# A hybrid decoder step on one core: the order of work at five places, and the sampled states' product with C on GpSimd

## What is computed

```python
def block(x, lp, past):
    x = x + 0.5 * swiglu(rmsnorm(x, lp["ffn1_norm"]), lp["ffn1_w_gate"], lp["ffn1_w_up"], lp["ffn1_w_down"])
    m, new_state = mix_layer(rmsnorm(x, lp["mix_norm"]), lp, past)
    x = x + m
    x = x + 0.5 * swiglu(rmsnorm(x, lp["ffn2_norm"]), lp["ffn2_w_gate"], lp["ffn2_w_up"], lp["ffn2_w_down"])
    return x, new_state
```

## Time and profile before

| | |
|---|---|
| median of three runs | 1480.89 us (1479.32 to 1481.51) |
| the profiled execution, its own time | 1479.76 us |
| its span, first to last instruction | 1477.7 us |
| PE busy | 1425.7 us, 96% |
| DVE busy | 802.8 us, 54% |
| ACT busy | 485.8 us, 33% |
| POOL busy | 194.6 us, 13% |
| chain that ended last | PE 83%, DVE 10%, ACT 3%, issue 2%, DMA 1% |

### The profile page before, as it was taken

The page is one execution under the profiler, slowest core; times in us unless marked ns, Lnnn a source line. Parts: engine busy times, 40 slices in busy tenths (PEclk is TensorE's granted clock), DMA queues, the critical chain, the costliest instruction groups (busy, mean ns, idle before and its releaser), DMA issues.

```text
span 1477.7 us, 28457 instructions
## 1 busy us (share of the span) xinstructions
PE 1425.7 (96%) x11676; PEld 1394.6 (94%) x11676; DVE 802.8 (54%) x983; ACT 485.8 (33%) x651; POOL 194.6 (13%) x187
## 2 busy tenths in 40 slices
PE   5999999999999999999999698999999999999999
PEld 5999999999999999999997688899999999999999
DVE  4444444333346557476787599885556564443222
ACT  5222232222243435342132464453332222322111
POOL 1000000010100000005700011210136750000000
PEclk9999999999999999999999899999999999999999
DMA  5232333333332313328956944556345543323332
GB/s 160 87 99 85 95 90 86 90 113 107 110 108 58 85 43 100 86 66 282 305 175 193 152 138 143 146 173 196 90 128 162 180 142 93 91 86 90 92 92 83
DMA packets 274776, 180.99 MB, mean 122 GB/s; under 512 B 13744, under 2 KB 253584, under 8 KB 274592
## 3 DMA queue, kind: packets, MB, share of 16 engines
q1 hardware_dynamic: 264512, 151.56, 36.1%
q0 software_dynamic: 6752, 22.27, 4.7%
q10 hardware_dynamic: 3456, 6.39, 1.2%
HBM read 162.42 MB, written 17.77 MB: 122 GB/s over the span
## 4 chain that ended last, share of the span: by engine, by line
PE 83%; DVE 10%; ACT 3%; issue 2%; DMA 1%; SPq 0%; DVEq 0%; ACTq 0%; POOL 0%; POOLq 0%
PE ps L442 75%; PE ps L1885 2%; DVE w_lo L423 2%; PE ps L1665 1%; PE ps L1675 1%; DVE gbuf L1294 1%; ACT w_hi L418 1%; PE ps L1681 1%; DVE hin L1283 1%; PE ps L1692 1%; DVE state L1306 1%; DVE ysm L1307 1%; DVE csb L1291 1%; DMA csb<-cs_kept 1%; PE ps L1797 0%
## 5 line engine op out<-in xcount | busy, mean ns | idle before, releaser
L442 PE MATMUL ps<-xg_hi,w_hi 128*128 128x260 f32 x2512 | 516.1, 287 | 22.2 <-DVE w_lo L423 21.7
L442 PE MATMUL ps<-xg_hi,w_lo 128*128 128x260 f32 x2512 | 508.4, 284 | 0.0
L442 PE MATMUL ps<-xg_lo,w_hi 128*128 128x260 f32 x2512 | 507.8, 284 | 0.0
L423 DVE TENSOR_TENSOR w_lo<-stage,w_hi 128x1024 fp32r<-128x1024 f32 (+1 forms) x229 | 302.0, 1319 | 264.1 <-ACT w_hi L418 260.2
L442 PEld LDWEIGHTS ps<-xg_hi,w_hi 128*128 128x128 f32 x2512 | 390.3, 190 | 28.1 <-issue 21.4
L442 PEld LDWEIGHTS ps<-xg_hi,w_lo 128*128 128x128 f32 x2512 | 389.6, 190 | 0.0
L442 PEld LDWEIGHTS ps<-xg_lo,w_hi 128*128 128x128 f32 x2512 | 389.3, 190 | 0.0
L418 ACT ACTIVATE w_hi<-stage 128x1024 fp32r<-128x1024 f32 (+1 forms) x229 | 237.3, 1036 | 330.0 <-PE ps L442 255.9
L442 PE MATMUL ps<-hid_hi,w_hi 128*128 128x260 f32 x704 | 141.9, 283 | 0.0
L442 PE MATMUL ps<-hid_hi,w_lo 128*128 128x260 f32 x704 | 141.5, 282 | 0.0
L442 PE MATMUL ps<-hid_lo,w_hi 128*128 128x260 f32 x704 | 141.3, 282 | 0.0
(11 more groups left out here) (299 smaller groups left out, 1451.0 us busy)
## 6 DMA issues: line engine op xcount, KB each, us to landing
stage<-in_w_in SPq DMA_DIRECT2D x69, 512.0 KB, 5.0
stage<-in_ffn_w_gate SPq DMA_DIRECT2D x44, 512.0 KB, 3.9
stage<-in_ffn_w_up SPq DMA_DIRECT2D x44, 512.0 KB, 3.8
stage<-in_ffn_w_down SPq DMA_DIRECT2D x32, 448.0 KB, 3.7
stage<-in_ffn_w_down SPq DMA_DIRECT2D x16, 512.0 KB, 3.9
pages<-in_cache_sb_k SPq DMA_DIRECT2D x32, 256.0 KB, 4.4
pages<-in_cache_sb_v SPq DMA_DIRECT2D x32, 256.0 KB, 3.6
gates<-gates_kept POOLq DMA_DIRECT2D x24, 260.0 KB, 4.1
```

What stands on the lines that cost most here:

```text
L423: nc.vector.tensor_tensor(w_lo[:, r, 0:kt, :], stage[:, s, 0:kt, :], w_hi[:, r, 0:kt, :].bitcast(F32), ALU.subtract).then_inc(unit_split, 1)
L442: mm = nc.tensor.matmul(out[:, h, :], wt[:, r, k, :], v[:, h * HALF:(h + 1) * HALF], start=start and k == 0 and n == 0, stop=stop and k == ...
```

## The change

- Start: SP raises its semaphores after the first loads are issued. PE runs 14 products of a matrix of ones into a bank that nobody reads, as soon as the constants stand. Unit 2 (`THIRD`) has weight buffers of its own, `w2_hi` and `w2_lo`, and is rounded before the squares; units 2 and 3 have accumulators in banks 6 and 4 of their own.
- Gates: POOL's product of a page with the query is two instructions of half the size. ACT loads the table of exponentials after the loop of gates, no longer ahead of it.
- Values: DVE copies `b_tok` one gate earlier, and takes `cb` ahead of the last convolution.
- Entry of SSD: POOL loads the decays of tile 0 earlier; ACT rounds the second unit of branch B ahead of the first decays; PE turns x after four row blocks of dense work, and does four more before the first chunk states.
- SSD loop: `csb` has three buffers, and a load runs three tiles ahead. POOL multiplies the sampled states with C; DVE waits for POOL (`state_weighted`) and only sums.

```diff
         def round_unit(u0, step, kt):
...
-            nc.scalar.wait_ge(unit_done, u0 + 1 + step)
-            nc.scalar.activation(w_hi[:, r, 0:kt, :], stage[:, s, 0:kt, :], ACT.Copy).then_inc(hi_ready, 1)
+            if u0 != THIRD:
+                nc.scalar.wait_ge(unit_done, u0 + 1 + step)
+            nc.scalar.activation(high(u0)[:, 0:kt, :], stage[:, s, 0:kt, :], ACT.Copy).then_inc(hi_ready, 1)
...
         def _(sp):
-            for s in signals:
-                sp.sem_inc(s.sem, s.n)
...
             for k in range(DT):
                 sp.dma_start(x[:, k, :], ins["x_t"][:, k, :]).then_inc(x_landed[k], 16)
...
+            for s in signals:
+                sp.sem_inc(s.sem, s.n)
...
-            act.preload_act_table_set("natural_log_exp_and_others")
             with act.Fori(0, NS // SLOTS) as i:
                 for b in range(SLOTS):
                     pass_gate(G_PRE + b, SLOTS * i)
+            act.preload_act_table_set("natural_log_exp_and_others")
...
             act.wait_ge(prep_d, 7)
+            round_unit(U_SSD + 1, 0, DT)
             decays(0, 0)
             decays(0, 1)
             for t in range(SSD_T):
                 it, u = t // 2, U_SSD + 3 * (t // 2)
-                round_unit(u + (1, 3)[t % 2], 0, DT)
+                if t:
+                    round_unit(u + (1, 3)[t % 2], 0, DT)
...
             def state_c(t):
-                dve.wait_ge(state_landed[t % 2], 16 * (t // 2 + 1))
-                dve.wait_ge(c_landed, 16 * (t // GT + 1))
-                link(nc.vector.tensor_tensor(state[t % 2][:, :, :], state[t % 2][:, :, :], cbb[:, :, :], ALU.mult))
+                dve.wait_ge(state_weighted, t + 1)
                 nc.vector.tensor_reduce(ysm[:, t, :], state[t % 2][:, :, :], AX_X, ALU.add).then_inc(state_used.sem, 1)
...
-                    nc.gpsimd.tensor_tensor(tiles, tiles, query.unsqueeze(1).broadcast_to([P, PAGES, SB_T, P]),
-                                            ALU.mult).then_inc(kq_ready.sem, 1)
+                    pair = [P, PAGES // 2, SB_T, P]
+                    for half in (tiles[:, 0:PAGES // 2], tiles[:, PAGES // 2:PAGES]):
+                        last = nc.gpsimd.tensor_tensor(half, half, query.unsqueeze(1).broadcast_to(pair), ALU.mult)
+                    last.then_inc(kq_ready.sem, 1)
...
             pool.wait_ge(cs_stored, 16)
+            load_cs(0)
             pool.wait_ge(pvd_done.sem, pvd_done.now(NS // SLOTS - 1, SLOTS - 1))
-            load_cs(0)
             load_cs(1)
+            load_cs(2)
             for t in range(SSD_T):
-                if t < SSD_T - 2:
+                pool.wait_ge(state_landed[t % 2], 16 * (t // 2 + 1))
+                pool.wait_ge(c_landed, 16 * (t // GT + 1))
+                nc.gpsimd.tensor_tensor(state[t % 2][:, :, :], state[t % 2][:, :, :], cbb[:, :, :], ALU.mult
+                                        ).then_inc(state_weighted, 1)
+                if t < SSD_T - 3:
                     pool.wait_ge(y_summed.sem, y_summed.now(0, t))
-                    load_cs(t + 2)
+                    load_cs(t + 3)
                 add_y(t)
...
             pe.wait_ge(consts_set, CONSTS)
+            for _ in range(14):
+                nc.tensor.matmul(ps[:, 7, 0:P], ones[:, :], ones[:, :], start=True, stop=True)
             ffn(1, U_FFN1A, O_FFN1A, U_FFN1B, O_FFN1B)
...
-            turn(0)
             for t in range(SSD_T):
                 dense(12 * t, 12 * t + 4)
                 if t == 0:
+                    turn(0)
...
                     mm.then_inc(v_summed, 1)
+                    dense(4, 8)
                 pe.wait_ge(xd_ready.sem, xd_ready.now(0, t))
```

More of the change, by code:

```diff
@@ L432, in multiply_unit @@
             if begin == 0:
-                if start:
+                if o0 == O_FFN1A + 3:
+                    nc.tensor.wait_ge(rms_ready, 1)
+                elif start and o0 != O_FFN1A + 2:
                     nc.tensor.wait_ge(acc_read, o0 + 1 + ostep)
@@ L439, in multiply_unit @@
                     nc.tensor.wait_ge(*ready(k))
-                for n, (wt, v) in enumerate(((w_hi, hi), (w_hi, lo), (w_lo, hi))):
+                for n, (wt, v) in enumerate(((hi_w, hi), (hi_w, lo), (lo_w, hi))):
                     for h in range(2):
-                        mm = nc.tensor.matmul(out[:, h, :], wt[:, r, k, :], v[:, h * HALF:(h + 1) * HALF],
+                        mm = nc.tensor.matmul(out[:, h, :], wt[:, k, :], v[:, h * HALF:(h + 1) * HALF],
                                               start=start and k == 0 and n == 0,
@@ L822, in decays @@
                 act.wait_ge(seg_ready.sem, seg_ready.now(0, h))
[L823 removed]
+                nc.scalar.activation(row, row, ACT.Exp).then_inc(ecs_ready.sem, 1)
                 nc.scalar.activation(gbuf[:, slot, :], gbuf[:, slot, :], ACT.Exp, scale=-1.0
@@ L1204, in _ @@
                     rest_unit(U_GATE + g + 1, SLOTS * i, DT)
+                    if i and b == 3:
+                        for k in range(GROUPS):
+                            dve.wait_ge(cb_made, k + 1)
+                            chunks = "p (c l) -> p c l"
+                            nc.vector.tensor_tensor(cb[:, k, :].rearrange(chunks, c=CH),
+                                                    ps[:, (6, 4)[k], :].rearrange(chunks, c=CH),
+                                                    upto[:, :].unsqueeze(1).broadcast_to([P, CH, P]), ALU.mult
+                                                    ).then_inc(cb_ready, 1)
                     t = ds(SLOTS * i + b, 1)
@@ L1290, in head @@
                 dve.wait_ge(ecs_ready.sem, ecs_ready.now(0, 2 * t + e))
-                nc.vector.tensor_tensor(csb[:, slot, :], csb[:, slot, :], ct[:, t // GT, :], ALU.mult
+                row = csb[t % 3][:, e, :]
+                nc.vector.tensor_tensor(row, row, ct[:, t // GT, :], ALU.mult
                                         ).then_inc(csc_ready.sem, 1)
@@ L1858, in _ @@
                         rows = slice(HD * e, HD * e + HD)
-                        mm = nc.tensor.matmul(ps[rows, 7, cols], hin[:, c, rows], csb[:, 2 * (t % 2) + e, cols],
+                        mm = nc.tensor.matmul(ps[rows, 7, cols], hin[:, c, rows], csb[t % 3][:, e, cols],
                                               start=False, stop=True)
```

73 lines of the change are left out of this document (41 added, 32 removed).

## The result

The changed kernel takes 1468.54 us (median of four runs, 1465.9 to 1469.91), the kernel before 1481.2 beside it: a ratio of 0.9913, 95% interval 0.989 to 0.9936. It is faster, by 12.7 us where 23 were forecast, and 1.5 us above the range's upper end. The profiled execution took 1469.0 us for a span of 1467.2; against that of before (1479.76, span 1477.7) it is 10.8 us shorter.

What follows compares the result with a forecast made beforehand. PE, busy 96% of the span, was bounded by few large waits, the SSD loop by DVE. Terms 9.2 + 4.5 + 13.5 - 4 = 23.2 us off gave 1457.5 us against the median, range 1447 to 1467.

Steps and rivals of the forecast that it cites:

- the range's upper end: Whole kernel: 1467 us, holding most of the exposed-product and moved-hole cases and adding the clock lost once or twice.
- Start: Start of the kernel: earlier loads, clock raised by ones, no hole before unit 2; 9.2 us off, bounds 6 and 11.
- the 1.2 for the ones: Start: products of ones raise PE's clock before the first unit; 1.2 us taken back of 2.3 lost.
- Gates: Loop of gates: the 3.15 us hole and half clock behind it go; 4.5 us off, bounds 1 and 5.
- Entry: Entry of SSD: PE's 10.86 us wait, smaller waits and half clock go, less a late head; 13.5 us off.
- What is late next is DVE's second head of tile 0: Entry of SSD: PE's next wait, its dense work ending about 1.2 us before that head.
- The prediction's own 1.2 us: Entry of SSD: PE's remaining wait for DVE's second head of tile 0, subtracted from the gain.
- The product: SSD loop: moving the product with C to POOL; 4 us on, bounds 10 off and 11 on.
- I take 1.7 us, two thirds: 1.7 - 1.22 = 0.5 a tile: SSD loop: exposed part of POOL's 2.6 us product, less DVE's saved 1.22 us; 4 us on in all.
- the rival to which 0.02 was given: SSD loop: PE standing 3 us or more every tile loses clock, 1.7 us per stretch, reaching 1484; chance 0.02.
- the prediction's own sign of being wrong: SSD loop: holes of 3 us with a clock of 0.5, or a pair of tiles at 25 us.

Runs made afterwards that it cites:

- the kernel with the product alone: The kernel before, with only the product with C moved to POOL, ahead of decay loads and addition of squares; 1487.19 us, ratio 1.0056.
- the kernel with the late outputs: SP's four convolution-state stores moved from SSD's entry to tiles 4, 5 and 6: 1467.63 us on the change alone, 1449.67 with POOL's product started by second heads.
- the product behind the heads: The change with POOL's product started by a tile's second head, two orders changed and DVE's stored-gates wait moved behind tile 0's heads; 1452.93 us.
- the missing ones: The change without the 14 products of ones at the start; 1473.6 us, ratio 0.9955.

## Why the prediction was wrong

It was right that the kernel gets faster and on two of four terms, and wrong by half on the sum.

*Start*, 9.2 forecast, 7.8 found. The hole before unit 2 and its half clock are gone, SP's first load is at 0.81, PE's first dense product at 8.70. The old start ends at 89.64 us and, in the kernel with the product alone, at 90.98; the new one at 81.15 to 82.49. So the gain is between 7.2 and 9.8, and the 9.2 is not shown to be off. What stays open is the 1.2 for the ones. In the change PE stood 1.5 us ahead of unit 1 at 11.18 and ran at half clock behind that (pairs of 0.64 us) in spite of the ones. In the kernel with the late outputs the clock stayed full, and PE stood 2.15 us at 22.47 for DVE's sums of squares: much of what PE gains there it waits for later.

*Gates*, 4.5 and 3.8: right, within its bounds. By the two kernels with the old gates (262.7 and 260.8 us) against the changed ones (258.1 to 259.0) it is 1.9 to 4.6; the two differ in whether the clock falls behind the hole. Halves still stretch remainders (3.1 and 3.4 us at 676.74 and 701.20), but PE waits for none longer than 0.8.

*Entry*, 13.5 and 5.4: the step that failed is "What is late next is DVE's second head of tile 0". The three links of the chain were moved, as said. Late next was the wait for the stored gates, which stood ahead of the remainder on DVE's queue all along, and PE's hole stayed at 7.1 us. It cost nothing before, since ACT was later. The working counted what the loads gain by going early, and not what stands behind them: a store that comes 2 us behind those loads takes 8 us longer to land than one that comes ahead of them. The prediction's own 1.2 us is there once that wait is gone: in the four kernels with the wait moved and no product of POOL beside the heads of tile 0, PE stands 1.17 or 1.18 us for the second head. With all that is late next removed in turn (the store's wait, the meeting with the first product, the four outputs), y of tile 1 comes 24.0 us earlier than before (825.46 against 849.41), of which start and gates are 11.7: 12.2, near the 13.5.

*The product*, +4 forecast, +9.1 found between the marks, and 12.2 against the same kernel without it. POOL's price was right: 2.35 to 2.87 us a product against 2.6. "I take 1.7 us, two thirds: 1.7 - 1.22 = 0.5 a tile" was the term that was mis-sized: 12.2 us over the seven tiles between the marks are 1.7 a tile, not 0.5, of which 1.0 is idle time of PE and 0.7 its lower clock. An average hid two things. The stalls come bunched: PE stands 2.8 to 3.9 us in tiles 2, 4, 6 and 7, and 0.6 or less in the others. And three of these holes fall, with half clock behind them, between the two marks. Against the kernel before, the waits and the clock make equal parts of the 9.1: 4.5 us of idle time and 4.6 of slower work. The prediction's term had no price for the clock; only its upper end added it once or twice. That is the mechanism of the rival to which 0.02 was given, in a milder form, and the prediction's own sign of being wrong: holes of 3 us in the loop with a clock of 0.5. The pairs of tiles take 29.3 and 30.4 us, where 28 to 29 stood. It was held against that rival that waits of 2.3 us had left the clock at 1.00; holes only half a microsecond longer lost it here.

Two roundings in the prediction are off and carry nothing: half of 4742 ns is 2.4 us, not 2.3, and 1456.6 and 1.1 make 1457.7.

The Trainium skill's SBUF page (SBUF — State Buffer, who interferes with whom) says that the loser of the shared ports blocks for the whole instruction, that a VectorE instruction with two inputs in SBUF contends with a GpSimd instruction that reads SBUF, and that one with at most one such input, outside certain fast modes, does not. The row at 843.55 (2.42 us for 0.68) and the rows of the product behind the heads (four instructions at their own length) agree on both sides.

*Behind the loop* 2.6 us more were gained than forecast, of which 1.1 are waits for DVE's merge (1.7 us in two before, 0.6 in one now). No run was made on it. From y of tile 7 to the end the thirteen profiled kernels take 542.5 to 545.9 us, and none of the experiments edits that part, so the 2.6 us are not clear of the spread.

## What to carry to other kernels

When two engines block each other as DVE and POOL do here, the price of work that moves between them is set by which instructions stand beside it, and its trigger decides that: started by the end of the last instruction that must not be blocked, with the two orders fitted to it, the same product went from a loss of 9.5 us to a gain of about 4. When a chain at a seam is shortened, list every wait on the queue of the engine that comes next, a store's landing included, and everything that the earlier transfers now overtake. And a stall that is averaged over tiles says little, where a bunched one can cost the clock as well.

## What was not expected of the hardware

- A store of 260 KB took 2.7 us to land when issued ahead of 2 MB of loads and 8.6 to 13.8 us in the kernels where it came 1 to 3 us behind the first of them, also between kernels that differ only at the start. In the profiled execution that is most of what made the missing ones look like a loss of 5 us.
- Four small stores (16 to 96 KB) held SP's queue for 0.7 to 4.3 us each at the entry, and for 0.6 to 1.9 us in later tiles. The expectation calls their elements 4 bytes; the trace does not show that. What it shows is 5472 packets under 512 bytes between 785 and 822 us, and 272 in the same stretch of the kernel that differs by the place of these stores alone.
- Half clock behind a hole was not a matter of its length alone. In the SSD loops of all thirteen kernels it came behind 10 of 10 holes of 3.9 us and more, 13 of 18 of 2.7 to 3.4 us, and 3 of 14 of 1.6 to 2.4 us. In one run 3.32 us at tile 0 left the clock at 1.00, and 2.11 us at the next tile was followed by 3.41 us at 0.50:

```profile
814.30:817.70 3.40, 3.40 (x45) 3.23 (x46) 3.33 (x5) 0.00 (x0) 1.11 (x2) 1.00 0.87 59
829.46:832.87 3.41, 3.41 (x26) 3.08 (x23) 3.34 (x4) 1.58 (x5) 2.96 (x3) 0.50 0.04 12
```
